# A hybrid decoder layer on one core: the samples' state readout taken out of the state-space groups

## The reference

```python
cb = jnp.einsum('blgn,bsgn->blsg', c_k, b_k)
y_diag = jnp.einsum('blsg,blsgh,bsghp->blghp', cb, decay, xdt_k)
y_off = jnp.einsum('blgn,bghpn->blghp', c_k, state) * jnp.exp(cum)[..., None]
...
y = y + lp['d_skip'].astype(jnp.float32)[:, None] * xh
y = y.reshape(b, L, D_INNER) * jax.nn.silu(z.astype(jnp.float32))
yg = y.reshape(b, L, SSD_GROUPS, D_INNER // SSD_GROUPS)
yg = yg * lax.rsqrt(jnp.mean(jnp.square(yg), axis=-1, keepdims=True) + RMS_EPS)
y = yg.reshape(b, L, D_INNER) * lp['ssd_norm_w']
branch_b = jnp.einsum('blc,cd->bld', y.astype(h.dtype), lp['w_ssd_br'])
merged = jax.nn.sigmoid(g_pool) * branch_a + jax.nn.sigmoid(g_ssd) * branch_b
```

## Time and profile before

| | |
|---|---|
| median of 3 runs | 2334.11 us (2332.47 to 2346.47) |
| the profiled execution's own span | 2344.2 us |
| PE busy | 2278.3 us, 97% |
| DVE busy | 1376.8 us, 59% |
| ACT busy | 1142.0 us, 49% |
| chain that ended last | PE 94%, DVE 3%, DMA 1%, ACT 1% |
| DMA | 447.38 MB, mean 191 GB/s |

### The profile page before, as it was taken

The page is one execution under the profiler, slowest core; times in us unless marked ns, Lnnn a source line. Parts: engine busy times, 40 slices in busy tenths (PEclk is TensorE's granted clock), DMA queues, the critical chain, the costliest instruction groups (busy, mean ns, idle before and its releaser), DMA issues.

```text
span 2344.2 us, 48620 instructions
## 1 busy us (share of the span) xinstructions
PE 2278.3 (97%) x18028; PEld 2247.6 (96%) x18028; DVE 1376.8 (59%) x2280; ACT 1142.0 (49%) x1603; POOL 117.2 (5%) x219
## 2 busy tenths in 40 slices
PE   7999999999999999999999999889999999999995
PEld 6999999999999999999999989789999999999995
DVE  6677667766777544444445653466666664444444
ACT  4555545545544544443344343257777764433332
POOL 1110001000100000000000000011111100000000
PEclk9999999999999999999999998789999999999998
DMA  6555545544545555555556554257878775555551
GB/s 248 194 195 182 180 148 200 183 172 164 202 136 194 185 178 177 179 177 178 179 179 213 184 192 148 90 196 273 286 269 290 266 262 179 179 180 180 172 181 63
DMA packets 120726, 447.38 MB, mean 191 GB/s; under 512 B 14648, under 2 KB 14712, under 8 KB 119096
## 3 DMA queue, kind: packets, MB, share of 16 engines
q1 hardware_dynamic: 99648, 362.92, 45.5%
q0 software_dynamic: 21008, 83.46, 10.8%
HBM read 423.67 MB, written 23.96 MB: 191 GB/s over the span
## 4 chain that ended last, share of the span: by engine, by line
PE 94%; DVE 3%; DMA 1%; ACT 1%; issue 0%; SPq 0%; POOL 0%; ACTq 0%; DVEq 0%; POOLq 0%
PE G L336 25%; PE G L337 25%; PE G L338 25%; PE M L336 3%; PE M L337 3%; PE M L338 3%; PE M L430 3%; PE M L558 1%; DMA sb_raw<-in_wstream 1%; PE G L607 1%; PE M L422 1%; DVE sb_resid L1517 1%; PE G L582 1%; PE M L444 1%; DVE sb_resid L1515 1%; DVE sb_wlo L1118 1%
## 5 line engine op out<-in xcount | busy, mean ns | idle before, releaser
L1118 DVE TENSOR_TENSOR sb_wlo<-sb_raw,sb_whi 128x1024 fp32r<-128x1024 f32 x688 | 834.6, 1223 | 837.5 <-ACT sb_whi L741 835.1
L741 ACT ACTIVATE sb_whi<-sb_raw 128x1024 fp32r<-128x1024 f32 x688 | 720.9, 1058 | 876.6 <-PE G L338 732.9
L336 PE MATMUL G<-sb_xH,sb_whi 128*128 128x264 f32 x3136 | 914.2, 292 | 28.6 <-DVE sb_wlo L1118 18.5
L337 PE MATMUL G<-sb_xL,sb_whi 128*128 128x264 f32 x3136 | 910.2, 290 | 0.0
L338 PE MATMUL G<-sb_xH,sb_wlo 128*128 128x264 f32 x3136 | 909.2, 290 | 0.0
L336 PEld LDWEIGHTS G<-sb_xH,sb_whi 128*128 128x128 f32 x3136 | 609.8, 194 | 30.9 <-issue 26.8
L337 PEld LDWEIGHTS G<-sb_xL,sb_whi 128*128 128x128 f32 x3136 | 607.7, 194 | 0.0
L338 PEld LDWEIGHTS G<-sb_xH,sb_wlo 128*128 128x128 f32 x3136 | 607.4, 194 | 0.0
L336 PE MATMUL G<-sb_hH,sb_whi 128*128 128x264 f32 x704 | 199.2, 283 | 2.2 <-issue 2.2
L337 PE MATMUL G<-sb_hL,sb_whi 128*128 128x264 f32 x704 | 200.2, 284 | 0.0
L338 PE MATMUL G<-sb_hH,sb_wlo 128*128 128x264 f32 x704 | 199.7, 284 | 0.0
(11 more groups left out here) (287 smaller groups left out, 3006.9 us busy)
## 6 DMA issues: line engine op xcount, KB each, us to landing
sb_raw<-in_wstream SPq DMA_DIRECT2D x688, 512.0 KB, 3.4
sb_resid<-in_state_T POOLq DMA_DIRECT2D x64, 256.0 KB, 4.9
sb_sq<-in_state_ssd POOLq DMA_DIRECT2D x32, 512.0 KB, 4.7
out_new_ssd_s<-sb_sq POOLq DMA_DIRECT2D x32, 512.0 KB, 3.8
sb_cumbc<-scr_cum POOLq DMA_DIRECT2D x8, 1024.0 KB, 4.9
sb_kc<-in_kc POOLq DMA_DIRECT2D x2, 2048.0 KB, 13.2
sb_vc<-in_vc POOLq DMA_DIRECT2D x2, 2048.0 KB, 8.7
sb_bcb<-scr_bc POOLq DMA_DIRECT2D x32, 128.0 KB, 6.2
```

The lines of the kernel that those rows point to most:

```text
L336: pe.matmul(out, w, kH, start=start, stop=False)
L337: pe.matmul(out, w, kL, start=False, stop=False)
L741: act.activation(whi[:, slot, :], raw[:, slot, :], ACT.Copy).then_inc(hi_ready, 1)
L1118: dve.tensor_tensor(wlo[:, slot, :], raw[:, slot, :], whi[:, slot, :].bitcast(F32), ALU.subtract)\
```

## The change

The groups do only the prompt's 256 columns after the convolution. They put aside what the samples need later: `dtxc`, `xsamp` (x), `zsamp` (the gated z), `bcp` (B times C), and the C rows, which TensorE transposes beside those of B and GpSimd writes to a new DRAM tensor `scr_cc`. `sample` and the loads of `state_T` go, and so does that input.

The readout is done in the first branch on VectorE. For each of 64 pairs of group and sample, one with each unit: `readout` multiplies a state row (`sS`, 256 KB, three buffers, from `state_ssd`, half of a 1024-column row) by the sample's C broadcast over partitions (`sC`, 64 KB, two buffers), then splits the unit, then sums over the 128 states into `CS`. GpSimd issues both loads for sample u when readout u - 2 is finished (`ss_used`). The first two wait for the last `mixL` of pooling.

At the start of the second branch the samples' y is put together for all groups at once, its mean square formed with one matmul between two units (`sample_squares`, behind unit q = 2 of the first block), and its high and low parts written into `yH`, `yL`; TensorE waits for that (`syl_ready`) before its second block.

```diff
-            def sample(b):
-
-                pe.wait_ge(s[f"st_in{b % 4}"], t[f"sti{b % 4}"].add() * 16)
-                for i in range(XPG):
-                    last = pe.matmul(M[3][:, 384 + i * NSAMP + b:385 + i * NSAMP + b], stT[:, b % 4, i * P:i * P + P],
-                                     CTt[:, SEQ + b:SEQ + b + 1], start=True, stop=True)
-                last.then_inc(s["st_used"], 1)
...
-                block_units(xH, xL, KT, SETS[1], between=lambda q: [head(2 * q), head(2 * q + 1), sample(2 * q),
-                                                                    sample(2 * q + 1)])
+                block_units(xH, xL, KT, SETS[1], between=lambda q: [head(2 * q), head(2 * q + 1)])
...
+                pe.transpose(M[2][0:NSAMP, 384:512], CTt[:, SEQ:T], ident[:, :]).then_inc(s["btok_ps"], 1)
...
+            def sample_squares(q):
+
+                if q == 2:
+                    pe.wait_ge(s["ssq_ready"], 1)
...
+            def y_complete():
+                pe.wait_ge(s["yl_ready"], YT)
+                pe.wait_ge(s["syl_ready"], 1)
...
+            branch(yH, yL, YT, between=sample_squares, ready=y_complete)
+            with rounds(pe, 7, t, dict(unit=12, sgm=2, br_read=2)):
+                branch(yH, yL, YT)
...
+                split(2 if samples else 4)
+                if samples:
+                    act.wait_ge(s["sy_ready"], 1)
+                    act.activation(sqs, CS[:, :, :], ACT.Square).then_inc(s["ssq_ready"], 1)
+                    split(2)
+                finished(4)
...
+            gate(samples=True)
+            act.wait_ge(s["ssq_ps"], 1)
+            act.wait_ge(s["sy_ready"], 2)
+            act.activation(srstd, srstd, ACT.Sqrt, scale=1.0 / (XPG * P), bias=eps[:, 0:1]).then_inc(s["ssd_ready"], 1)
...
+            def readout(u):
+
+                dve.wait_ge(s[f"ss_in{u % 3}"], t[f"ssi{u % 3}"].add() * 16)
+                dve.wait_ge(s[f"sc_in{u % 2}"], t[f"sci{u % 2}"].add() * 16)
+                dve.wait_ge(s["ss_used"], START["ss_used"] + t["row"].now())
+                done = mark(dve.tensor_tensor(prod[:, :, :], sS[u % 3].rearrange("p (i n) -> p i n", i=XPG),
+                                              sC[u % 2].rearrange("p (o n) -> p o n", o=1).to_broadcast([P, XPG, P]), ALU.mult))
+                split(1)
+                after(done)
+                dve.tensor_reduce(flat(CS[:, bass.ds(t["row"].add() - 1, 1), :]), prod[:, :, :], AX_X, ALU.add)\
+                   .then_inc(s["ss_used"], 1)
...
+                for u in range(8):
+                    readout(u)
...
+            split(1)
+            samples_y()
+            split(3)
+            samples_mean()
+            samples_low()
+            split(8)
+            merge()
...
-                for b in range(4):
-                    load_state(b)
...
-                for b in range(4, NSAMP):
-
-                    alone(s["st_used"], g * NSAMP + (b - 3))
-                    load_state(b)
...
+                pool.dma_start(scr_cc[bass.ds(g * NSAMP, NSAMP), :], bcs[:, P:2 * P]).then_inc(s["bc_out"], 16)
...
+            def load_sample(row, pair, half, u):
+                pool.dma_start(sS[u % 3], a["state_ssd"][bass.ds(pair, 1), :, half * XPG * P:(half + 1) * XPG * P]
+                               .rearrange("g p c -> (g p) c")).then_inc(s[f"ss_in{u % 3}"], 16)
+                pool.dma_start(sC[u % 2], scr_cc[bass.ds(row, 1), :].to_broadcast([P, P])).then_inc(s[f"sc_in{u % 2}"], 16)
...
+            pool.wait_ge(s["mix_lo"], 2 * KT)
+            for u in range(2):
+                load_sample(u, u // 2, u % 2, u)
+            with rounds(pool, GROUPS - 1, t, {}) as g:
+                for u in range(2, NSAMP + 2):
+
+                    alone(s["ss_used"], g * NSAMP + (u - 1 + START["ss_used"]))
+                    load_sample(g * NSAMP + u, g * 4 + u // 2, u % 2, u % NSAMP)
```

More of the change, by code:

```diff
@@ L912, in _, with gate @@
                     high(e)
[L914 to L932, removed]
+            def gate(samples=False):
+                split(2 if samples else 4)
[4 more added lines that the diff above has]
+                finished(4)
+                act.wait_ge(s["br_read"], START["br_read"] + t["br"].now())
+                for j in range(2):
+                    act.activation(sgA[:, j, :], SETS[0][j][:, 0:T], ACT.Sigmoid).then_inc(s["sgm"], 1)
+                t["br"].add(2)
@@ new lines, in merge @@
+            def merge():
+                split(8)
+                t["done"].add(8)
+                i = t["mf"].now()
+                for j in range(2):
+                    act.wait_ge(s["br_read"], START["br_read"] + t["br"].now(1 - j))
+                    act.activation(flat(mixH[:, bass.ds(i + j, 1), :]), tmp[:, j, :], ACT.Copy)\
+                       .then_inc(s["mix_hi"], 1)
+                t["mf"].add(2)
+            with rounds(act, 8, t, dict(unit=8, done=8, br=2)):
+                gate()
+                split(4)
+                t["done"].add(4)
@@ L934, in _ @@
+            with rounds(act, 7, t, dict(unit=12, done=12, br=2, mf=2)):
+                gate()
+                merge()
             for b in range(8):
@@ new lines, in per_tile, with by_group, per_sample @@
+            def per_tile(name):
+                at = VEC_AT[name]
+                return vec[:, at:at + YT].rearrange("p (g o i) -> p g o i", o=1, i=XPG).to_broadcast([P, GROUPS, NSAMP, XPG])
+            def by_group(x):
+                return x[:, :, :].rearrange("p (g b) i -> p g b i", g=GROUPS)
+            def per_sample(x):
+                return x.rearrange("p (s o) -> p s o", o=1).to_broadcast([P, SG, XPG])
+            with rounds(dve, 8, t, dict(unit=8, done=8, sg=2, br=2, step=8, row=8, ssi0=3, ssi1=3, ssi2=2, sci0=4, sci1=4)):
+                for u in range(8):
+                    readout(u)
+                i = t["br"].now()
+                dve.wait_ge(s["sgm"], START["sgm"] + t["sg"].add(2))
+                finished(8)
+                for j in range(2):
+                    dve.tensor_tensor(flat(resid[:, bass.ds(i + j, 1), :]), SETS[1][j][:, 0:T], sgA[:, j, :], ALU.mult)\
+                       .then_inc(s["br_read"], 1)
+                    t["br"].add()
@@ L1454, in residual @@
+            split(1)
[3 more added lines that the diff above has]
+            samples_low()
+            split(8)
+            merge()
+            with rounds(dve, 7, t, dict(unit=12, done=12, sg=2, br=2, step=2, mh=2)):
+                split(12)
+                merge()
             def residual(b, units, first=0, sets=2, parts=False):
```

219 lines of the change are left out of this document (120 added, 99 removed).

## The result

The changed kernel takes 2362.7 us, the median of 4 runs (2361.7 to 2372.3), against 2334.7 for the median of 4 runs of the kernel before. The ratio is 1.012, with a 95% interval of 1.009 to 1.015: about 28 us slower. The forecast was 2338 us, with a range of 2288 to 2395. The time lies in the range, 25 us above the number and 0.7 above the 2315 to 2362 that the prediction gave its central case.

The account below looks back on a forecast made before the run. TensorE was taken to bound the kernel; groups -84.5, first branch +72.7 and tail +15.6 sum to +3.8 us, put on the median of 2334.1 to give 2337.9 us, range 2288 to 2395.

Parts of the forecast that it names:

- central case: Whole kernel: 2338 us, own range 2315 to 2362, with a state-to-C-row latency of 4.8 us; chance 0.42.
- L: First branch: time from the state load's issue to the C row's landing, taken as 4.8 us.
- rival 2: First branch: loads as slow as in the FFN, 2360 us at its best pair, 2402 at its median; chance 0.22.
- groups: Group stages: sample blocks and 18 slow stretches go, a transpose and some VectorE waiting come; -84.5 us.
- first branch: Readouts beside TensorE's units: the loop of loads two samples ahead takes longer than TensorE's units; +72.7 us.
- tail: Start of the second branch: TensorE idles 5.7 and 6.9 us, plus 3.0 of slow clock; +15.6 us.
- Rival 3: Groups: heads alone trigger the slow stretches, so these stay; +28 us, 2366; chance 0.07.
- P: First branch: time of one loop from readout finished to readout finished, L + 3.4, 8.2 us for two samples.
- the FFN pair's best: First branch: latency bound from the FFN's fastest state and broadcast pair, 5.5 us, scaled to 3.9 to 4.7.
- VectorE as the bound: First branch: product and sum take 1.3 of VectorE's 1.7 us idle per unit, so they cost nothing.
- rival 5: First branch: the loop of loads doesn't bind at all, 2265 us; wants L under 2.4; chance 0.03.
- rival 4: First branch: TensorE's clock falls as it waits; two slow stretches per pair of units cost about 26 us, 2364; chance 0.07.

Follow-up runs that it names:

- run 8: The kernel before, unchanged, profiled three more times: 16, 18 and 23 slow stretches in the groups, spans 2340.7, 2339.8 and 2347.8 us.
- Run 7: The kernel before with the sample block's 512 matmuls moving 64 columns instead of one, into one PSUM place: 2316.0 us, ratio 0.990.
- run 1: The changed kernel with the branch's loads done once ahead of the loop, all 64 products and sums kept: 2273.9 us, ratio 0.972.

## Why the prediction was right or wrong

The mechanism was right: the groups give back what was forecast, and a loop of loads two samples ahead bounds the branch. The forecast was 25 us low, and the miss has two halves. It also ended at an edge: the measured L is 5.4 us, where the prediction put the border between its central case and rival 2 (loads as slow as in the FFN), and rival 2's 2360 us are nearer to the 2363 than the forecast, in part by chance, since they carry the same low base.

**The base, 12.4 us.** The prediction summed the change against the profiled execution and then took the sum off the median of the runs, since "nothing in it scales". The profiled execution was the slowest of the three, 2346.5 us, the median 2334.1. But 27.7 us of the gain were the removal of 18 slow stretches, counted in that slow execution. A quicker execution with fewer stretches has less to lose. Off the execution's own time the same sum gives 2346.5 + 3.8 = 2350.3. This is the step that failed first: a sum read from one execution was taken off another's time, though part of it are events whose number changes between them. How much of the 12.4 us is owed to the stretches is not shown. That the quicker executions had fewer of them is argued from their clocks (run 8). A further execution with 18 stretches took 2341.4 us, 5 less than this one, and this one had 5 us more in attention and 1.5 in pooling that have nothing to do with the change. The median of the first three runs was also low: on the later occasions it was 2338.2 and 2341.6.

**The sum, 12.5 us.** 2362.8 - 2346.5 = 16.3 against +3.8. By its terms, read at the first output of the out projection (1256.6 before, 1276.3 after) and, for the groups, at the end of pooling:

| term | predicted | measured |
|---|---|---|
| groups | -84.5 | -84.1 |
| first branch | +72.7 | +87.1 |
| tail | +15.6 | +16.7 |
| rest of the program | 0 | -3.1 |
| sum | +3.8 | +16.6 |

The prediction counts the branch up to the end of TensorE's unit behind the last readout, taken as 2.94 us after that unit's split. These rows give it, the split in the changed kernel and, in the kernel before, the unit after that one:

```profile
969.38 0.69 DVE L1466 TENSOR_TENSOR sb_prod<-sb_tmp,sb_total 128x512 f32<-128x512 f32 x1
969.99 1.22 DVE L1155 TENSOR_TENSOR sb_wlo<-sb_raw,sb_whi 128x1024 fp32r<-128x1024 f32 x1
...
971.15 0.28 PE L336 MATMUL G<-sb_yH,sb_whi 128*128 128x264 f32 x1
```

The split ends at 971.21, so the unit would end at 974.15, which is 1058.2 on the clock of the kernel before, 84.1 later. Before it ended at 971.15: 87.1 us. The tail is what is left of 19.7: 19.7 + 84.1 - 87.1 = 16.7.

- *Groups.* Blocks of 59.7 us and 18 stretches of 1.54: right to 0.4 us. Rival 3, that heads alone keep the stretches, is refuted by the clock of 1.00. Run 7 divides the term: the wide matmuls take away the stretches and leave the blocks. A group takes (591.61 - 148.06) / 6 = 73.93 us there and 66.63 in the changed kernel, 58.4 over eight groups, where blocks less transposes are 59.7 - 0.9 = 58.8. The first group of the changed kernel takes 68.1, and those 1.5 us are all that is seen of the 2 for VectorE.
- *The loop.* The mechanism, its place and three of its four terms were right. Finished to issue 0.74 in the median (0.79 predicted), landing to product 0.11 (0.2), product, split and sum 2.42 (2.42). The term that was mis-sized is L: 5.4 instead of 4.8. It is 0.58 to the issue of the C row and 4.83 to its landing, the median of the 31 C rows whose wait closes the loop; over all 64 it is 4.6, but the others are hardly waited for. The terms add up to 0.74 + 5.41 + 0.11 + 2.42 = 8.68, and the loop measures 8.70, where P was 8.2. That is 0.5 on P, 31 x 0.5 = 15.5 us; the first turn began 1.4 earlier than forecast (readout 1 finished at 702.0, 786.1 on the clock of the kernel before, against 787.5), which leaves 14.1 of the 14.4 us. The choice between the bounds is what missed. The bound from the FFN pair's best was 3.9 to 4.7, that from its median 5.2 to 6.0; the measured 5.4 lies in the second. A loop of 31 turns pays the median, and of the transfers that it waits for.
- *Who is awaited.* VectorE waits for the C row, 118.2 us in 34 waits, not for the state, as forecast. That the state's latency rises too, from 3.6 alone to 4.5, was not.
- *VectorE as the bound* at no cost: right (run 1). *It doesn't bind* (rival 5): right only without the loop. Four buffers come near the 2265 us of that case (2271.7), which carries the same error in the base.
- *Tail.* Its two waits are 2.9 and 7.2 us, where 5.7 and 6.9 stood. The first is short only as idle time: the unit ahead of it, begun at 968.80, ran into a slow stretch and took 4.5 us instead of 2.9. From the end of the split, 971.21, to the start of the squares at 976.37 it is 5.2. The other 4.3 us, where 3.0 stood, are about the matmul of the squares, 0.7, which the sum left out, and the slow clock behind the waits, 1.4 and 2.2 by the starts of the units. With four buffers the first wait is gone and the second stays.
- *Clock in the branch* (rival 4). There were 14 slow stretches in the branch, one for about two turns, such as 952.5 to 955.9 with a clock of 0.50. The loop's terms hold no work of TensorE and add up without them, so I take them as covered by the waits; no run tested that alone.
- *Rest.* TensorE gains 4.6 us in the attention stage and loses 1.5 to a slow stretch at 2198. The further profiles of the kernel before (run 8) differ from the first by as much, so no effect of the change can be told from the variation between executions.

The timeline of TensorE at the two waits of the tail, and the start of the unit ahead of the first:

```profile
968.80 0.39 PE L348 MATMUL G<-sb_xH,sb_whi 128*128 128x264 f32 x1 [1.82 <-DVE sb_wlo L1155]
976.37 1.22 PE L536 MATMUL M<-sb_prod,sb_ones 128*128 128x256 f32 x2 [2.87 <-ACT sb_prod L934]
988.69 0.56 PE L348 MATMUL G<-sb_yH,sb_whi 128*128 128x264 f32 x1 [7.16 <-DVE sb_yL L1520]
```

So the change is sound in the groups and spoilt in the branch by how far ahead it loads. It takes 84 us of TensorE's time off the groups, and gives 87 back in the branch, since a load issued two samples ahead closes a loop of 8.7 us in a stage that has 5.9 for it, and 17 more in the tail.

## What to carry to other kernels

When work moves off the bounding engine onto operands that stream in, sum the whole loop (release, issue, latency, use) and divide it by the samples in flight; compare that with the engine's time per unit before comparing any busy shares. Release a buffer at its last reader, not at the end of the task: one moved count was worth 64 us here, and loading four samples ahead instead of two 91. And ask of each gain whether it is there in every execution, before a sum made on one profile is taken off a median.

## What the runs showed of the hardware

- A load of 64 KB as one row broadcast to 128 partitions took as long as one of 256 KB: 3.5 and 3.6 us in the median with only the weight stream beside it, 4.6 and 4.5 when issued 0.58 us apart.
- Behind 16 to 23 of the 32 sample blocks, each 16 records of one column, TensorE's clock fell to the 1.2 GHz level. With 64 columns in the same matmuls it fell behind none, and a block took 1.80 us where it had taken 1.81. The kernel was 1.0% faster so (0.990, 0.987 to 0.994); a version that moves needless columns and keeps its results right was not run.
- A product of 128x512 into PSUM took 0.70 us against 0.69 into SBUF, a sum from it 0.684 against 0.679.
